# A single-core encoder step whose opening is rebuilt: turned inputs, sums of squares as products, a halved first quarter

## The chip, the core and the metric

The kernel runs on one core of one Trainium2 chip. The metric is the time on the device in microseconds, from the start of the program to its end; lower is better.

## What is computed

One layer of a streaming encoder over 384 rows (256 of a prompt, 8 x 16 of samples) of width 2048. Cut to what the change touches:

```python
mod = einsum('bd,de->be', silu(c), w_ada) + b_ada        # c: 9 rows of 2048; w_ada: 2048 x 6144
shift, scale, gate = split(mod, 3)
h = rmsnorm(x, ln_gain) * (1 + scale[:, None]) + shift[:, None]
proj = einsum('btd,de->bte', h, w_in)                    # then latent attention, sparse attention,
out = einsum('bte,ed->btd', y, w_out)                    # gated norms, and the output projection
```

So every product with `w_in` needs h, and the quarter of h for 512 columns of the model width needs the shift and scale of those columns. Such a quarter takes all 2048 rows of `w_ada`, for 512 columns of the shift and 512 of the scale.

## The kernel before

All weights are streamed from HBM once, packed on the host into "units" of 128 partitions x 1024 floats (512 KB). `units()` writes out by hand the order in which TensorE works through them; `loads()` gives the order of their transfers, all issued by SyncE (SP) on one queue. A unit of the modulation goes into a ring of 8 slots (`araw`), every other one into a second ring of 8 (`raw`); SP waits, in order, until the slot's earlier unit has been used.

- Modulation units ("ada"): 16 per quarter of the width, four quarters. A unit is one 128-row block (kt) of `w_ada` with 512 columns of shift and 512 of scale; TensorE multiplies the silu of c with it (`products`, L1761, 4 matmuls of 256 columns, which the trace shows as 8 records).
- Dense units ("kb", the keys; "ga", the gates of group A; "ckv" and so on): columns of `w_in`. Each is split into a high and a low part: ScalarE copies it to `w_hi` (L957), VectorE subtracts (L1280), and TensorE multiplies high by high, high by low and low by high, with h split the same way: 18 matmuls of 512 columns for a key unit (L1780), 24 of 384 for a gate unit (L1791). Splits are written three units ahead in ScalarE's and VectorE's programs.
- Between the modulation units of the second to fourth quarter stand three or four dense units each, so that TensorE has work while w_ada streams. A key unit of index k covers the width blocks 2k and 2k+1 and needs h of those; a "ga" unit covers four blocks.

`plan()` hangs further steps on the units, in the same order on every engine. At the end of a quarter q: `modT` (ScalarE copies the bank into `modA`, TensorE turns it, VectorE adds the bias, L1326 to L1330), then `h` for its two pairs of blocks (VectorE L1342 for the samples, ScalarE L1039 for the prompt, then the copy to `hT_hi`), then `hl` (`hT_lo`, L1351). `hT_ready` counts the finished blocks and the early key and gate units wait for it. Each engine runs its own program strictly in this order.

The opening. SP first issues c (two transfers), an identity matrix, and x in three transfers of 1 MB with rows on partitions; then the units. GpSimd issues six small loads, the gains among them. TensorE turns c; ScalarE takes its silu into `cs`. ScalarE and VectorE each square half of every row tile with a running sum (`xsq`); `xr` forms 1/rms with row-wise scalars, a diagonal of it times a matrix of ones spreads it over the partitions (`rb`, L1827), and then TensorE turns x in twelve steps of four blocks (L1836), one between any two modulation units, and VectorE multiplies each with 1/rms on its way to `xsT` (L1310). A last small transposition brings the gains into `gcol`.

## Time and profile before

| | us |
|---|---|
| median of 3 runs | 921.27 (920.39 to 922.1) |
| the profiled execution, its own time | 921.53 |
| its span (first to last instruction) | 919.7 |
| TensorE busy | 885.2 (96%) |
| VectorE, ScalarE, GpSimd busy | 413.8, 321.7, 121.8 |

The span is what the trace covers; 1.8 us of the execution lie around it. Times in rows are from the span's start. The page gives shares over the whole span; what bounds a stretch is read from the timeline and the waits of that stretch. In the timeline a row is one instruction or several equal ones in sequence (x8 is eight records), and the bracket tells how long the engine had stood idle and who released it.

### The profile page before, as it was taken

The numbers are of one execution on the slowest core, as the hardware profiler recorded it, in microseconds if no ns is written. First come the engines' busy times: TensorE is split into PE (matmuls) and PEld (weight loads), VectorE is DVE, ScalarE is ACT, GpSimd is POOL, SyncE is SP. The second block draws the span as 40 slices with busy tenths as digits, with TensorE's granted clock in tenths as the row PEclk, the third lists the DMA queues.
The fourth block names the chain that finished last, engine by engine and source line by source line (L and its number), as shares of the span: only waits on it lengthen the run. The fifth ranks groups of instructions, "written<-read, shape, count | busy, mean of one in ns | idle before, by whom it ended". The sixth has DMA issues, their size and how long they took to land.

```text
span 919.7 us, 13678 instructions
## 1 busy us (share of the span) xinstructions
PE 885.2 (96%) x5533; PEld 766.1 (83%) x5533; DVE 413.8 (45%) x850; ACT 321.7 (35%) x600; POOL 121.8 (13%) x192
## 2 busy tenths in 40 slices
PE   3799999999999999999999999999999999999996
PEld 1376788999998688888999888888988899778886
DVE  3522343336422145443332476138645466677362
ACT  3222343333421234222331353234234345554252
POOL 1000003101200000112220400003002224440000
PEclk9799999999999999999999999999999999999999
DMA  8999957475443222556552667547878843793413
GB/s 339 409 408 409 407 199 221 157 238 168 150 136 105 69 75 86 172 165 238 166 157 88 216 228 248 185 159 218 315 246 254 262 141 110 264 303 120 138 53 131
DMA packets 53599, 187.43 MB, mean 204 GB/s; under 512 B 7872, under 2 KB 8568, under 8 KB 52384
## 3 DMA queue, kind: packets, MB, share of 16 engines
q1 hardware_dynamic: 39488, 141.32, 43.7%
q0 software_dynamic: 13904, 44.71, 15.2%
q8 instruction: 44, 0.72, 0.3%
q10 hardware_dynamic: 144, 0.52, 0.1%
q14 instruction: 19, 0.16, 0.1%
HBM read 175.93 MB, written 12.69 MB: 205 GB/s over the span
## 4 chain that ended last, share of the span: by engine, by line
PE 82%; DVE 3%; ACT 2%; issue 1%; POOL 0%; DVEq 0%; ACTq 0%; POOLq 0%
PE proj L1791 33%; PE proj L1780 27%; PE proj L1810 2%; PE proj L1761 2%; PE bankO L1889 2%; PE bankO L1898 1%; PE bankS L1810 1%; DVE w_lo L1280 1%; PE bankS L1952 1%; PE bankO L1979 1%; PE bankO L1971 1%; PE bankO L1970 1%; PE bankO L1939 1%; PE bankS L1780 1%; PE bankS L1995 1%
## 5 line engine op out<-in xcount | busy, mean ns | idle before, releaser
L1280 DVE TENSOR_TENSOR w_lo<-raw,w_hi 128x1024 fp32r<-128x1024 f32 (+2 forms) x164 | 197.5, 1211 | 239.7 <-ACT w_hi L957 239.0
L957 ACT ACTIVATE w_hi<-raw 128x1024 fp32r<-128x1024 f32 (+2 forms) x164 | 167.2, 1026 | 183.7 <-PE proj L1780 104.3
L1791 PE MATMUL proj<-hT_hi,w_hi 128*128 128x384 f32 x608 | 210.7, 347 | 0.0
L1791 PE MATMUL proj<-hT_hi,w_lo 128*128 128x384 f32 x608 | 203.7, 335 | 0.0
L1791 PE MATMUL proj<-hT_lo,w_hi 128*128 128x384 f32 x608 | 203.4, 335 | 0.0
L1780 PE MATMUL proj<-w_hi,hT_hi 128*128 128x512 f32 (+2 forms) x464 | 178.5, 385 | 2.3 <-DVE w_lo L1280 1.5
L1780 PE MATMUL proj<-w_hi,hT_lo 128*128 128x512 f32 (+2 forms) x464 | 174.1, 375 | 0.0
L1780 PE MATMUL proj<-w_lo,hT_hi 128*128 128x512 f32 (+2 forms) x464 | 173.9, 375 | 0.0
L1791 PEld LDWEIGHTS proj<-hT_hi,w_hi 128*128 128x128 f32 x608 | 114.2, 188 | 9.4 <-issue 8.2
L1791 PEld LDWEIGHTS proj<-hT_lo,w_hi 128*128 128x128 f32 x608 | 114.3, 188 | 0.6 <-issue 0.2
L1791 PEld LDWEIGHTS proj<-hT_hi,w_lo 128*128 128x128 f32 x608 | 114.1, 188 | 0.0
L1780 PEld LDWEIGHTS proj<-w_hi,hT_hi 128*128 128x128 f32 x464 | 87.6, 189 | 19.9 <-DVE w_lo L1280 4.4
L1780 PEld LDWEIGHTS proj<-w_hi,hT_lo 128*128 128x128 f32 x464 | 87.4, 188 | 14.9
L1780 PEld LDWEIGHTS proj<-w_lo,hT_hi 128*128 128x128 f32 x464 | 87.7, 189 | 14.5 <-issue 0.7
L1761 PE MATMUL bankO<-araw,cs 128*32 128x256 f32 x512 | 36.7, 407 | 14.8 <-DMA araw<-in_units 13.7
L1761 PEld LDWEIGHTS bankO<-araw,cs 128*32 128x32 f32 x512 | 13.8, 112 | 30.5 <-issue 15.9
L1090 ACT ACTIVATE probs<-probs,stat 128x128 f32<-128x128 f32 (+2 forms) x40 | 17.7, 442 | 58.0 <-DVE stat L1412 49.4
L957 ACT ACTIVATE stage<-proj 128x384 f32<-128x384 f32 (+1 forms) x26 | 12.4, 538 | 28.2 <-PE proj L1791 11.9
L1402 DVE COPY knT<-bankO 128x256 f32<-128x256 f32 x8 | 3.4, 425 | 33.9 <-PE bankO L1889 33.9
L1506 DVE COPY qlT<-bankO 128x512 f32<-128x512 f32 x8 | 5.5, 692 | 29.1 <-PE bankO L1971 29.1
L929 POOL DMA_DIRECT2D out_k_p<-stage x2 | 1.5, 750 | 127.6 <-ACT stage L957 127.6
L1761 PE MATMUL proj<-raw,cs 128*32 128x256 f32 x256 | 18.2, 387 | 0.0
(371 smaller groups left out, 1036.2 us busy)
## 6 DMA issues: line engine op xcount, KB each, us to landing
raw<-in_units SPq DMA_DIRECT2D x184, 512.0 KB, 3.6
araw<-in_units SPq DMA_DIRECT2D x64, 512.0 KB, 9.1
kcT<-in_dsa_k_t POOLq DMA_DIRECT2D x8, 512.0 KB, 5.9
vc<-in_cache_dsa_v POOLq DMA_DIRECT2D x8, 512.0 KB, 5.0
gate_scratch<-stage POOLq DMA_DIRECT2D x8, 384.0 KB, 3.3
raw<-in_units SPq DMA_DIRECT2D x8, 336.0 KB, 4.4
raw<-in_units SPq DMA_DIRECT2D x8, 320.0 KB, 4.5
x_sb<-in_x_prompt SPq DMA_DIRECT2D x2, 1024.0 KB, 6.8
```

The costliest lines, as they stand in the source:

```text
L957: return nc.scalar.activation(out, in_, func, scale=scale, **kw)
L1090: ins = nc.scalar.activation(probs[:, e, p0:p0 + w], probs[:, e, p0:p0 + w] if src is None else src, ACT.Exp, bias=stat[:, 32 + 2 * e + s0 ...
L1280: V.tensor_tensor(w_lo[:, SLOT[u], 0:w], raw_of(u)[:, 0:w], high(u)[:, 0:w].bitcast(F32), ALU.subtract).then_inc(lo_ready, 1)
L1761: ins = mm(banks[0][32 * g:32 * (g + 1), 0:256], cs[:, k, :], cols, start=first, stop=final)
L1780: ins = mm(banks[t][:, 0:ncol], a[:, kt, rows], w[:, n, :], start=first and n == m == 0, stop=final and n == per - 1 and m == 2)
L1791: ins = mm(banks[blk][:, 0:TOK], w[:, n, cols], a[:, kt, :], start=first and n == m == 0, stop=final and n == per - 1 and m == 2)
L1810: ins = mm(out[:, part], a[:, kt, rows], w[:, n, part], start=k == n == m == 0, stop=last and n == 1 and m == 2)
L1889: ins = mm(out[:, 0:SEQ], wukT[:, h_ % 2, q, :], ckvT[:, q, 0:SEQ], start=q == 0, stop=q == CB - 1)
L1898: ins = mm(out[:], ckvT[:, q, P * t:P * (t + 1)], wuvT[:, q, 512 * g:512 * (g + 1)], start=q == 0, stop=q == CB - 1)
L1939: ins = mm(out[:, P * q:P * (q + 1)], wuk[:, h_ % 2, P * q:P * (q + 1)], qnT[:, h_, SEQ:TOK], start=True, stop=True)
L1952: mm(out[:, 0:NKEY], qlT[:, q, b, :], ckvcT[:, b % 3, q, :], start=q == 0, stop=False)
L1970: mm(out[:, cols], ckvc[:, b % 4, cols], probsT[:, b % 2, 0:P], start=True, stop=False)
```

## The change

- x and c are laid out turned on the host (model width on partitions). x comes in four transfers of 768 KB straight into `xsT`, after one for c; the identity and the gains, now turned too, follow behind the second unit. GpSimd's four loads of gains go; its last two wait until x has landed. TensorE's turning of c, of x (48 transpositions) and of the gains goes.
- The sums of squares: ScalarE and VectorE square the 16 blocks (1536 or 768 elements at a time, `xsq`), TensorE adds them up by 16 products with ones in four column groups (`xss`), VectorE copies, one more product with ones spreads the sum (`rb`), ScalarE takes the root of 128 x 384 and VectorE the reciprocal of 128 x 384. x is then scaled by pairs of blocks (`xm`, 8 instructions of 128 x 768 on VectorE) between the other steps.
- The first quarter of the modulation is cut into two halves ("ade", 8 units each, each unit two row blocks by 256 + 256 columns). `modT`, `h` and `hl` follow each half with one pair of blocks; the first pair can so be ready after 8 units.
- The two "ga" chunks of the opening become one, "gp", of 8 units of two row blocks by 512 columns, with four banks.
- The order of units: dense units stand now at positions 10, 14, 22 and 29 of the first 36 (from 0), where they stood at 20, 25, 30 and 35. From position 36 on the kinds stand as before, a "gp" for each "ga". Dense units are loaded 3 or 4 positions early, not 6. In `loads()` the last modulation unit is number 76 (from 0) both times.

The diff, cut to its core ("..." marks what is left out):

```diff
...
-MQ = 4
+MODS = [("ade", 0), ("ade", 1), ("ada", 1), ("ada", 2), ("ada", 3)]
+MOD_BLOCKS = [(0, 2), (2, 4), (4, 8), (8, 12), (12, 16)]
+MOD_OF_PAIR = [0, 1, 2, 2, 3, 3, 4, 4]
...
-    out = [("ada", q, 1, 1) for q in range(4)]
-    out += [("kb", 0, 2, NT), ("ga", 0, 4, 2), ("ga", 1, 4, 2), ("ckv", 0, 2, NT), ("m0", 0, 2, NT), ("m1", 0, 2, NT)]
+    out = [("ade", e, 2, 1) for e in range(2)] + [("ada", q, 1, 1) for q in range(1, 4)]
+    out += [("kb", 0, 2, NT), ("gp", 0, 2, 4), ("ckv", 0, 2, NT), ("m0", 0, 2, NT), ("m1", 0, 2, NT)]
...
-    keys, first, second = of("kb", 0), of("ga", 0), of("ga", 1)
-    out = of("ada", 0)
-    for q in range(1, 4):
-        ada = of("ada", q)
-        out += ada[:4] + [keys[2 * q - 2]] + ada[4:8] + [first[q - 1]] + ada[8:12] + [keys[2 * q - 1]] + ada[12:]
-        out.append(second[q - 1])
-    out += [keys[6], keys[7], first[3], second[3]]
+    keys, gates = of("kb", 0), of("gp", 0)
+    half = of("ade", 1)
+    out = of("ade", 0) + half[:2] + [keys[0]] + half[2:5] + [gates[0]] + half[5:]
+    ada = of("ada", 1)
+    out += ada[:4] + [keys[1]] + ada[4:10] + [gates[1]] + ada[10:]
+    for q in range(2, 4):
+        ada, n = of("ada", q), 2 * q - 2
+        out += ada[:4] + [keys[n]] + ada[4:8] + [gates[n]] + ada[8:12] + [keys[n + 1]] + ada[12:] + [gates[n + 1]]
+    out += [keys[6], keys[7], gates[6], gates[7]]
...
-    for u in [u for u in order if CHUNKS[UNITS[u][0]][0] != "ada" and u < last + 3]:
+    first = UNITS.index((CHUNK_OF["ade", 1], 0))
+    second = UNITS.index((CHUNK_OF["ada", 1], 0))
+    last = UNITS.index((CHUNK_OF["ada", 3], KT - 1))
+    for u in [u for u in order if CHUNKS[UNITS[u][0]][0] not in ("ade", "ada") and u < last + 3]:
         at = order.index(u)
         order.remove(u)
-        order.insert(max(first, at - AHEAD), u)
+        order.insert(max(first, at - (3 if u < second else 4)), u)
...
+        return [u + LEAD] if u + LEAD != FIRST_UNIT["kb", 0] else []
...
+        elif kind == "gp":
+            mine = [3, 4, NPB + 1, NPB + 2]
...
-    put(0, ("xsq", 0), ("xsq", 1), ("xsq", 2), ("xr", 0))
+    put(0, ("xsq", 0), ("xsq", 1), ("xsq", 2), ("xsq", 3))
+    put(0, ("xss", 0), ("xss", 1), ("xss", 2), ("xss", 3))
     put(1, ("rb", 0))
-    run(1, "xT", 6, 2)
-    run(2, "xS", 6, 2)
-    put(13, ("gains", 0))
-
-    for q in range(4):
-        u = LAST_UNIT["ada", q]
-        put(u, ("modT", q))
-        for kind in ("h", "hl"):
-            put(u, (kind, 2 * q), (kind, 2 * q + 1))
+    put(4, ("xm", 0))
+    put(9, ("xm", 1))
+    for m in range(2, 8):
+        put(8 + 2 * m, ("xm", m))
+
+    for n, mod in enumerate(MODS):
+        u = LAST_UNIT[mod]
+        pairs = [m for m in range(KT // 2) if MOD_OF_PAIR[m] == n]
+        put(u, ("modT", n))
+        if n == 0:
+            put(u, ("first_hi", 0))
+        put(u, *(("h", m) for m in pairs))
...
+        put(u, *(("h", m) for m in pairs))
+        if n == 0:
+            put(u, ("first_lo", 0))
+        put(u, *(("hl", m) for m in pairs))
...
-        sp.dma_start(c_rows[:, 0, :], i["c_sample"].rearrange("j (k p) -> (j k) p", p=P)).then_inc(sem("c_in"), 16)
-        sp.dma_start(c_rows[0:KT, 1, :], i["c_prompt"].rearrange("j (k p) -> (j k) p", p=P)).then_inc(sem("c_in"), 16)
-        sp.dma_start(eye[:], i["c_eye"]).then_inc(sem("eye_in"), 16)
-        for t in range(NT):
-            sp.dma_start(x_sb[:, t, :], x_rows[0][:, t] if t < 2 else x_rows[1]).then_inc(sem(f"x_in{t}"), 16)
-        for u in LOADS:
+        sp.dma_start(c_sb[:], i["c_t"]).then_inc(sem("c_in"), 16)
+        for at_, u in enumerate(LOADS):
+            for n in {0: (0, 1, 2, 3)}.get(at_, ()):
+                blocks = slice(4 * n, 4 * n + 4)
+                sp.dma_start(xsT[:, blocks, :], i["x_t"][:, blocks, :]).then_inc(sem(f"x_in{n}"), 16)
+            if at_ == 1:
+                sp.dma_start(eye[:], i["c_eye"]).then_inc(sem("eye_in"), 16)
+                sp.dma_start(gcol[:], i["gains_t"]).then_inc(sem("gains_in"), 16)
...
-            load(gains_in[0:16, :], i["ln_gain"][0].rearrange("(k p) -> k p", p=P), "small_in")
-            load(gains_in[16:24, :], i["out_gain_a"][0].rearrange("(k p) -> k p", p=P), "small_in")
-            load(gains_in[24:32, :], i["out_gain_b"][0].rearrange("(k p) -> k p", p=P), "small_in")
-            load(gains_in[32:64, :], i["b_ada"][0, 0:2 * D].rearrange("(k p) -> k p", p=P), "small_in")
+            pool.wait_ge(sem("x_in3"), 16)
...
+        def xsq(n):
+            if n != 1:
+                blocks = slice(4 * n, 4 * n + (2 if n == 3 else 4))
+                act.wait_ge(sem(f"x_in{n}"), 16)
+                copy(xsqr[:, blocks, :], xsT[:, blocks, :], func=ACT.Square).then_inc(sem(f"x_sq{n}"), 1)
+
+        def rb(n):
+            filled(act, "rb", n)
+            nc.scalar.activation(rbc[:], bank["T"][:, 0:TOK], ACT.Sqrt, scale=1.0 / (32 * D),
+                                 bias=stat[:, 62:63]).then_inc(free["T"], 1)
+
+        def first_hi(_):
...
+            act.wait_ge(sem("x_scaled"), m + 1)
...
-        copy(cs[:, :, 1:9].rearrange("p k j -> p j k"), bank["S"][:, 0:P].rearrange("p (j k) -> p j k", k=KT),
-             func=ACT.Silu)
-        copy(cs[:, :, 0], bank["S"][:, P:P + KT], func=ACT.Silu).then_inc(sem("cs_ready"), 1)
+        copy(cs[:, :, 0:1 + DB], c_sb[:], func=ACT.Silu).then_inc(sem("cs_ready"), 1)
...
+        def xss(n):
+            if n < 3:
+                return
+            filled(dve, "xss", n)
+            V.tensor_copy(xsum[:], bank["S"][:, 0:TOK]).then_inc(free["S"], 1)
 
         def rb(n):
-            filled(dve, "rb", n)
-            V.tensor_copy(rbc[:], bank["S"][:, 0:TOK]).then_inc(free["S"], 1)
-
-        def turned(kind, n, b, i):
-
-            t, g = i % NT, i // NT
-            emptied(dve, "rb", 0)
-            filled(dve, kind, n)
-            V.tensor_tensor(xsT[:, 4 * g:4 * g + 4, P * t:P * (t + 1)], bank[b][:].rearrange("p (k q) -> p k q", q=P),
-                            rbc[:, P * t:P * (t + 1)].unsqueeze(1).broadcast_to([P, 4, P]),
-                            ALU.mult).then_inc(free[b], 1)
-
-        def xT(n):
-            turned("xT", n, "T", 2 * n)
-
-        def xS(n):
-            turned("xS", n, "S", 2 * n + 1)
+            emptied(dve, "rb", n)
+            link(V.reciprocal(rbc[:], rbc[:]))
+
+        def xm(m):
+            part = xsT[:, 2 * m:2 * m + 2, :]
+            V.tensor_tensor(part, part, rbc[:].unsqueeze(1).broadcast_to([P, 2, TOK]),
+                            ALU.mult).then_inc(sem("x_scaled"), 1)
+
+        def first_lo(_):
+            split(FIRST_UNIT["kb", 0])
...
+            if (kind, j) in MODS[1:] and first:
+                emptied(pe, "modT", MODS.index((kind, j)) - 1)
+            if kind == "gp" and first:
+                emptied(pe, "xss", 3)
+                emptied(pe, "rb", 0)
...
+                for n, g in itertools.product(range(2), range(4)) if kind == "ade" else ():
+                    cols = raw_of(u).rearrange("p (a n) -> p a n", a=2)[:, n, P * g:P * (g + 1)]
+                    ins = mm(banks[0][32 * g:32 * (g + 1), 0:P], cs[:, 2 * k + n, :], cols, start=first and n == 0,
+                             stop=final and n == 1)
...
+        def xss(n):
+            out = take("xss", n, "S")
+            pe.wait_ge(sem(f"x_sq{n}"), 2 if n == 3 else 1)
+            for g in range(4):
+                ins = mm(out[32 * g:32 * (g + 1), 0:TOK], ones[:, 0:32], xsqr[:, 4 * n + g, :], start=n == 0,
+                         stop=n == 3)
+            if n == 3:
+                ins.then_inc(full["S"], 1)
+
...
+            emptied(pe, "xss", 3)
+            mm(take("rb", n, "T")[:, 0:TOK], ones[:], xsum[:], start=True, stop=True).then_inc(full["T"], 1)
...
+    x = np.concatenate([inputs["x_prompt"][0], inputs["x_sample"].reshape(P, D)])
+    c = np.concatenate([inputs["c_prompt"], inputs["c_sample"]])
+    gains = np.concatenate([inputs["ln_gain"][0], inputs["out_gain_a"][0], inputs["out_gain_b"][0],
+                            inputs["b_ada"][0, 0:2 * D]])
+    return {"x_t": x.reshape(TOK, KT, P).transpose(2, 1, 0),
+            "c_t": c.reshape(1 + DB, KT, P).transpose(2, 1, 0),
+            "gains_t": gains.reshape(-1, P).T,
```

## Rows read from the trace of the kernel before

**Rows 1.** The page: the chain that ended last, its share by engine.
```profile
PE 82%; DVE 3%; ACT 2%; issue 1%; POOL 0%; DVEq 0%; ACTq 0%; POOLq 0%
```

**Rows 2.** The chain that ended last, in order: start, us, engine and line.
```profile
97.91 4.38 PE proj L1780 x18
...
117.51 2.11 PE bankS L1791 x12
...
139.40 40.60 PE proj L1780 x198
```

**Rows 3.** Engines by stretch: busy us (instructions), granted clock, DMA share, GB/s.
```profile
9.00:10.00 1.00, 0.00 (x0) 0.00 (x0) 0.00 (x0) 0.00 (x0) 0.00 (x0) 1.00 1.10 311
...
80.00:100.00 20.00, 18.77 (x162) 13.98 (x161) 8.32 (x13) 7.11 (x10) 0.00 (x0) 1.00 1.03 408
...
120.00:140.00 20.00, 20.00 (x100) 17.31 (x99) 6.68 (x7) 9.73 (x15) 2.23 (x4) 1.00 0.45 145
```

**Rows 4.** Timeline, ScalarE: start, us, what, [idle before <-releaser]; weight splits that waited for loads.
```profile
46.49 1.06 ACT L957 ACTIVATE w_hi<-raw 128x1024 fp32r<-128x1024 f32 x1 [3.46 <-DMA raw<-in_units]
...
114.45 1.06 ACT L957 ACTIVATE w_hi<-raw 128x1024 fp32r<-128x1024 f32 x1 [7.87 <-DMA raw<-in_units]
```

**Rows 5.** Timeline of the opening, several engines, same columns.
```profile
2.10 0.91 SPq L688 DMA_DIRECT2D x_sb<-in_x_prompt  x2
...
13.34 1.06 ACT L1024 ACTIVATE sqx<-x_sb 128x1024 f32<-128x1024 f32 x1 [1.18 <-DMA x_sb<-in_x_sample]
...
14.73 2.27 PE L1761 MATMUL bankO<-araw,cs 128*32 128x256 f32 x16 [10.50 <-DMA araw<-in_units]
...
18.61 0.56 DVE L1303 COPY rbc<-bankS 128x384 f32<-128x384 f32 x1 [2.37 <-PE bankS L1827]
19.36 0.64 PE L1761 MATMUL bankO<-araw,cs 128*32 128x256 f32 x8
...
35.02 0.64 PE L1761 MATMUL bankO<-araw,cs 128*32 128x256 f32 x8 [0.64 <-DMA araw<-in_units]
```

**Rows 6.** Timeline from the end of the second quarter's modulation to the next key unit.
```profile
63.84 0.38 ACT L957 ACTIVATE modA<-bankO 128x256 f32<-128x256 f32 x1 [9.68 <-PE bankO L1761]
...
65.31 1.68 DVE L1342 TENSOR_TENSOR xsT<-xsT,modT 128x256 f32<-128x256 f32 x4
...
67.45 0.96 DVE L1351 TENSOR_TENSOR hT_lo<-xsT,hT_hi 128x768 fp32r<-128x768 f32 x1 [0.45 <-ACT hT_hi L957]
...
70.23 2.36 DVE L1280 TENSOR_TENSOR w_lo<-raw,w_hi 128x1024 fp32r<-128x1024 f32 x2
...
71.51 0.50 PE L1780 MATMUL proj<-w_hi,hT_hi 128*128 128x512 f32 x1 [0.76 <-DVE w_lo L1280]
```

**Rows 7.** Granted clock by stretch, around its fall and its rise.
```profile
36.00:37.00 1.00, 0.45 (x2) 0.20 (x2) 0.32 (x3) 0.11 (x1) 0.00 (x0) 0.73 0.99 397
46.00:47.00 1.00, 1.00 (x4) 0.84 (x3) 0.00 (x0) 0.51 (x1) 0.00 (x0) 0.65 1.04 410
```

**Rows 8.** Timeline of TensorE between the first dense units.
```profile
37.62 1.08 PE L1761 MATMUL bankO<-araw,cs 128*32 128x256 f32 x8 [1.01 <-DVE modT L1326]
...
43.70 0.80 PE L1780 MATMUL proj<-w_hi,hT_hi 128*128 128x512 f32 x1
...
49.42 1.93 PE L1761 MATMUL bankO<-araw,cs 128*32 128x256 f32 x32
...
51.28 0.44 PE L1791 MATMUL proj<-hT_hi,w_hi 128*128 128x384 f32 x1
...
55.65 1.93 PE L1761 MATMUL bankO<-araw,cs 128*32 128x256 f32 x32
```

**Rows 9.** Timeline much later: a root, a reciprocal and 16 small matmul records of the same shapes.
```profile
534.92 0.58 ACT L1162 ACTIVATE rstd_y<-bankO,stat 128x384 f32<-128x384 f32 x1 [2.90 <-PE bankO L1985]
...
535.60 2.55 DVE L1523 RECIPROCAL rstd_y<-rstd_y 128x384 f32<-128x384 f32 x1 [1.85 <-ACT rstd_y L1162]
...
693.42 0.64 PE L2078 MATMUL bankO<-vc,probsT 128*32 128x128 f32 x16
```

More of the change, by code:

```diff
@@ L400, in packed_units @@
         dst = out[u, :, 0:per * n].reshape(P, per, n)
-        if kind == "ada":
+        if kind == "ade":
+            for a in range(2):
+                dst[:, :, 256 * a:256 * (a + 1)] = w_ada[:, ks, a * D + 256 * j:a * D + 256 * (j + 1)]
+        elif kind == "ada":
             for a in range(2):
@@ L1009, in evict @@
                 ins.then_inc(proj_free[b], 1)
-        def gains(n):
-            filled(act, "gains", n, "S")
-            copy(gcol[:], bank["S"][:, 0:64]).then_inc(free["S"], 1)
         def bias(n):
@@ L1195, in kl @@
                  bank["T"][:].rearrange("p (h s) -> p h s", s=P)).then_inc(free["T"], 1)
-        steps = {"gains": gains, "bias": bias, "xsq": xsq, "xr": xr, "h": h, "ckn": ckn, "ckT": ckT,
+        steps = {"bias": bias, "xsq": xsq, "rb": rb, "first_hi": first_hi, "h": h, "ckn": ckn, "ckT": ckT,
                  "kiT": kiT_,
@@ L1314, in xT, with xsq @@
-        def xT(n):
-            turned("xT", n, "T", 2 * n)
-        def xS(n):
-            turned("xS", n, "S", 2 * n + 1)
+        def xsq(n):
+            if n % 2:
+                blocks = slice(4 * n + (2 if n == 3 else 0), 4 * n + 4)
+                part = xsT[:, blocks, :]
+                dve.wait_ge(sem(f"x_in{n}"), 16)
+                V.tensor_tensor(xsqr[:, blocks, :], part, part, ALU.mult).then_inc(sem(f"x_sq{n}"), 1)
+        def xss(n):
[3 more added lines that the diff above has]
+            V.tensor_copy(xsum[:], bank["S"][:, 0:TOK]).then_inc(free["S"], 1)
@@ L1320, in modT_ @@
+        def rb(n):
+            emptied(dve, "rb", n)
[5 more added lines that the diff above has]
+        def first_lo(_):
+            split(FIRST_UNIT["kb", 0])
         def modT_(n):
             filled(dve, "modT", n)
-            part = modT[:, :, MQ * n:MQ * (n + 1), :]
@@ L1784, in products @@
             else:
-                for blk in range(2):
+                for blk in range(nb):
                     cols = slice(P * blk, P * (blk + 1))
@@ L1854, in ckT @@
             if t == 0:
-                moved(pe, "ga", 1)
+                moved(pe, "gp", 0)
             out = take("ckT", t, "T")
```

151 lines of the change are left out of this document (50 added, 101 removed), and 2 rows, old and new, of the table STEP_BANKS.

## Prediction, made before the changed kernel ran

> **What bounds the kernel now.** I read the page's chain first, then the chain in order of time, then the stretches, and then the timeline of the opening. The chain is TensorE for 82% [rows 1]. From 97.91 on it is TensorE almost without a break, and from 117.51, the first dense unit behind the last modulation unit, it runs on into 40 us of key-like units and so to the end [rows 2]. A time won or lost before 117.5 therefore comes out at the end one for one, as the stretch from 120 on shows: TensorE busy for 20.00 of 20 us, the transfers at 45% [rows 3]. What is left to ask is when the last modulation unit can be done.
>
> In the opening two things run neck and neck. The transfers stand at 408 GB/s, full, while TensorE is busy for 18.77 of 20 us [rows 3]. Landings can be read where ScalarE waits for a weight: load number 24 (from 0) at 46.49, number 77 at 114.45, so one unit per 1.282 us, and number 76, the last modulation unit, at 113.2 [rows 4]. TensorE finishes it at about 116.6, 2.9 us after landing plus its own half microsecond. So even before, TensorE and not the stream sets the end of this stage, by about 3 us. Of TensorE's own time there: a key unit 4.3 us at full clock [rows 2], a gate unit 4.36 (51.28 to 55.65), four modulation units with their gap 1.86 (49.42 to 51.28) [rows 8].
>
> TensorE begins its first key unit only at 43.70. Until 14.7 it has nothing, then its 20 modulation units come as fast as they land, between the turning of x.
>
> **The change, part by part.**
>
> The start of the stream. x is issued at 2.10 and its last third is there at 13.34, 11.24 us later; the first unit 1.36 after that [rows 5]. After, x goes out behind one transfer instead of three, near 1.15 (issues are 0.4 to 0.5 apart by the same row), so it lands near 12.4. The microsecond from 9 moved 311 GB/s and not 408 [rows 3]; if the small tables that GpSimd loads beside it are the cause, moving them saves 0.2 to 0.4. I take x at 12.0 (bounds 11.2 and 12.8), unit 0 at 13.4. The identity, gains and tables (some 0.16 MB) come later and take 0.4 at 408 GB/s, so later units land 1.0 earlier than before. Number 7 landed at about 24.2 (14.7 plus 7 times 1.355, the spacing up to number 15 at 35.02 [rows 5]), after: 23.2, and number 8 at 24.5. Bounds of this term: 0 to 2 us earlier.
>
> Turning x, c and the gains. 48 transpositions and three small ones leave TensorE, all before 33 us. They stand in a time in which it waits for units anyway: worth nothing by themselves. The cover is the landing of the units, and it stays.
>
> The new norm. Squares of the last x blocks: one instruction of 768 elements, near 0.96 as VectorE's of that size in rows 6, so 13.0. TensorE takes unit 0 first, then the 16 products with ones. Nothing shows this form of 384 columns in four column groups; the bounds are the 8 records of unit 0 at half and at full clock (1.08 and 0.5 to 0.64 per set of 256 columns [rows 5, 8]), times 1.5 and four sets: 3.0 to 6.5. The engine worked from 14.73 to 19.36 before an 8-record unit ran at 0.64 and not 1.1, so I take 5.0: 19.5. Then VectorE's copy 0.56 [rows 5], the spreading product 0.8 (estimated from the same 256-column records), the root of 384 columns 0.58, the reciprocal of 384 columns 2.55 [rows 9], the first scaling 0.96: 25.0. The cost of a reciprocal over 384 columns in place of 3 is 2.4 us, and it lies right beside the modulation's chain, below, so it costs nothing to 0.5.
>
> The first half. Number 7 at 23.2, its products 0.5, then bank, transposition and modulation: 1.47 for a full quarter (63.84 to 65.31 [rows 6]), 1.3 for a half: ready at 25.0. ScalarE has the high part of the first key unit ahead of h (`first_hi`): landed 24.5, 1.06 long [rows 4], 25.6. Then h and the high part, 2.14 (65.31 to 67.45), and `hT_lo` 0.96 [rows 6]: the first key unit can start at 28.7, where before it was 43.70. That is the gain of the change, 15.0 us, and the rest of the sum is what takes it back.
>
> The order behind it. Both kernels have four dense and 32 modulation units among the first 36, and the same kinds from number 36 on. So I follow TensorE to the key unit at position 40, which starts at 71.51 before [rows 6]; what comes after it is equal.
> - First key unit: 28.7. Before, it ran at the half clock for its first part and took 5.7 (43.70 to 49.42 [rows 8]), 1.4 over the full speed. The granted clock had fallen to 0.50 (1.2 GHz) at 36.5, after a stretch in which TensorE was busy for about half of the time, waiting for units; it came back to 1.00 (2.4 GHz) within 46 to 47 [rows 7]. After, the engine is still idler before 28.7. So 5.7: 34.4.
> - Three half-quarter units: 16 records each; such a set took 0.64 [rows 9]; 1.6 with the gap: 36.0. Gate unit 4.36: 40.4. Three more: 42.0.
> - Modulation of the second half 1.3: 43.3. The four units behind it (1.9) are all the work that TensorE now has, for the key unit at position 22 needs this h: 2.14 + 0.96, then one `xm` of 0.96 that stands ahead of its split on VectorE, then the split, 1.2 (half of 2.36 [rows 6]): 5.3. It starts at 48.6. TensorE is idle for some 4 of the 6.6 us since 42.0, less busy than in the stretch that lost the clock before [rows 5, 7], so it starts at half clock: 5.7, 54.3.
> - Six units 2.8, gate unit 4.36, six units 2.8: 64.3. Loads: number 35 is there at 46.49 + 11 x 1.282 - 1.0 = 59.6, early enough.
> - Modulation 1.5, 65.8, and 6.2 from there to the key unit (65.31 to 71.51 [rows 6]): 72.0. Before, this same chain ran under a gate unit, 4.36, and the four units; the new order has only the four. Another 7.7 us with 2.3 of work, another start at half clock, 1.4 again.
>
> In all 72.0 + 1.4 against 71.51: 1.9 us later. How long a rise takes is not one number: 1.4 of loss here, and from 14.73 to 19.36 [rows 5] 4.6 us at half speed, which is 2.3 of loss. I take 1.6 for each of the three, 0.6 more in all: **2.5 us slower**. Bounds: 1.9 - 1.0 (start of the stream at its best) to 1.9 + 2.7 + 1.0.
>
> On this point the Trainium skill has a rule that speaks against the change: "TensorE: Matmul & The Clock Gate", section "HAM oscillation — how this bites in real kernels", says that waits between bursts of matmuls throttle the engine anew, so that each burst begins slow. By that rule both new gaps cost a slow start, as in the sum; by the rows alone one could also hope that the 2 us of products inside each gap hold the clock, which would make the sum about 3 us less.
>
> The rest. Behind position 75 the order is the same. "gp" is evicted in one go with four copies; its wait for the keys' store on ScalarE is one where there were two, and TensorE stood at nothing there: its row from 139.40 is unbroken [rows 2]. Nothing, either way (bounds -0.3 to 0.3). Loads 3 or 4 early in place of 6: a split wants 2.3 us, and TensorE lags the loads by more; nothing. While TensorE is in a gap, the 8 slots stay full and SP waits, so the stream may pause for 1 to 2 us; the last modulation unit lands at 112.2 to 114.2, and TensorE comes to it near 119: covered.
>
> **The sum.** 921.53 (the profiled execution; the median of the runs is 0.26 below it) + 2.5 = 924.0.
>
> **The rivals.**
> - The clock holds in the gaps. For it: the three waits of 0.5 to 0.8 at the ends of the old quarters [rows 6] did not lose it. Against: those were short. Then two starts cost nothing: 924.0 - 3.2 = 920.8.
> - The early start pays. TensorE keeps most of its lead of 15 us (the chains to h are shorter than I make them, or dense work fits in), and the stream becomes the bound: the last modulation unit lands at 112.2, done at 112.7 and not 116.6: 917.6. This is the other side, faster; it decides as soon as the second and third chains are 4 us shorter or covered. For it: a full stream from 10 to 118. Against: in the new order nothing dense stands under either chain.
> - The rises are slow. All three as from 14.73: 0.7 more each, 2.1; and if the norm's chain (reciprocal) ends last, 0.5 more: 926.6.
> - The change does not reach the end at all, because gain and gaps cancel by chance: 921.5.
>
> **How the numbers follow.** Forecast (922.6 to 925.4) 0.40; clock holds 0.20; early start pays 0.18; slow rises 0.15; cancels 0.07. A measurement of this kernel tells about 0.2% from no change, 1.8 us: faster is below 919.4, slower above 923.1. Slower: 0.29 of the forecast and all of the slow rises, 0.44. Faster: 0.17 of the early start and 0.04 of the clock case, 0.21. The rest, 0.35, is the same. The range goes from 917.5 to 927.5: it takes in all cases but the best part of the early start (up to 0.1) and what goes beyond the slow rises (up to 0.08).
>
> **What the profile will show.** The first key unit at 28 to 29.5 (before 43.70). Two gaps on TensorE, near 44 to 49 and 66 to 72, with a `w_lo` split as releaser of the key unit that ends each. PEclk at 0.50 in both gaps and into the key units behind them, whose first products last 0.63 and not 0.39. ScalarE's waits for loads shifted by about -1. The key unit at position 40 at 71.5 to 74. If the gaps are there and the clock is 1.00 in them, the first rival holds; if the key units follow without a gap, my reading of the order is wrong, and the time falls to the stream's bound. If TensorE waits for loads in the third quarter, the stream's pause was under-priced.

## The result, and the profile after

The changed kernel takes 924.28 us (median of nine executions), the kernel before 921.27 beside it (nine, 920.39 to 922.1). The ratio is 1.0026, 95% interval 1.0015 to 1.0036, which is 2.4 us; the two medians lie 3.0 us apart. It is slower by 0.26%, just beyond the 0.2% that can be told from no change; the forecast was 924.0. Its executions took 922.11 to 925.27, but for one in a slow state (1116.97), and such ones are left out of all ratios. The profiled execution took 924.28 with a span of 922.4, where before's had 919.7.

The page's shares of the chain by engine, to be read against [rows 1]:

```profile
PE 82%; DVE 3%; ACT 2%; issue 1%; POOL 0%; ACTq 0%; POOLq 0%; DVEq 0%
```

Nothing of the difference is to be seen there. It is in the chain in order of time (start, us, what):

```profile
100.62 4.38 PE proj L1782 x18
...
142.12 40.60 PE proj L1782 x198
```

The block of 40.60 us is as long as before and starts 2.72 us later [rows 2]; so does the key unit at position 60 (100.62, 2.71 later). The span is 2.7 longer. So all of the loss stands before 100, and it reaches the end one for one. The timeline of the opening, from the first unit to the end of the third key unit, and then ScalarE at the end of the modulation:

```profile
13.20 1.08 PE L1756 MATMUL bankO<-araw,cs 128*32 128x128 f32 x16 [13.20 <-DMA araw<-in_units]
...
14.02 5.21 PE L1828 MATMUL bankS<-xsqr,ones 128*32 128x384 f32 x32
...
21.47 2.55 DVE L1308 RECIPROCAL rbc<-rbc 128x384 f32<-128x384 f32 x1 [1.62 <-ACT rbc L1039]
...
24.93 0.26 DVE L1326 TENSOR_TENSOR modT<-bankO,gcol 128x18 f32<-128x18 f32 x2
...
28.66 0.47 PE L1782 MATMUL proj<-w_hi,hT_hi 128*128 128x512 f32 x1 [0.55 <-DVE hT_lo L1350]
...
42.97 1.93 PE L1763 MATMUL bankO<-araw,cs 128*32 128x256 f32 x32 [0.35 <-DVE modT L1326]
...
48.30 0.50 PE L1782 MATMUL proj<-w_hi,hT_hi 128*128 128x512 f32 x1 [3.40 <-DVE w_lo L1290]
...
54.22 2.80 PE L1763 MATMUL bankO<-araw,cs 128*32 128x256 f32 x48
...
69.92 0.94 PE L1763 MATMUL bankO<-araw,cs 128*32 128x256 f32 x8 [0.63 <-DMA araw<-in_units]
...
71.85 0.79 PE L1782 MATMUL proj<-w_hi,hT_hi 128*128 128x512 f32 x1 [0.99 <-DVE w_lo L1290]
...
78.52 1.93 PE L1763 MATMUL bankO<-araw,cs 128*32 128x256 f32 x32
...
117.40 1.06 ACT L969 ACTIVATE w_hi<-raw 128x1024 fp32r<-128x1024 f32 x1 [5.32 <-DMA raw<-in_units]
119.35 0.38 ACT L969 ACTIVATE modA<-bankO 128x256 f32<-128x256 f32 x1 [0.89 <-PE bankO L1763]
```

The first key unit starts at 28.66, where it was 43.70 [rows 8]: a lead of 15 us. The next two stand behind waits for their own low part (48.30, and 71.85 where it was 71.51 [rows 6]). The third begins with a record of 0.79 us and takes 6.67 (71.85 to 78.52): the lead is gone, and more. "The first gap" below is the wait before 48.30, "the second gap" the waits before 71.85. The same stretches by engine (columns as in [rows 3]):

```profile
29.00:30.00 1.00, 1.00 (x4) 0.83 (x3) 0.56 (x2) 0.79 (x1) 0.00 (x0) 0.58 1.01 401
45.00:48.00 3.00, 0.00 (x0) 0.00 (x0) 2.72 (x3) 2.18 (x3) 0.00 (x0) 1.00 1.03 414
49.00:50.00 1.00, 1.00 (x6) 0.77 (x5) 1.00 (x3) 0.00 (x0) 0.00 (x0) 0.82 1.06 430
50.00:51.00 1.00, 1.00 (x4) 0.80 (x3) 1.00 (x1) 0.00 (x0) 0.00 (x0) 0.50 1.04 418
53.00:54.00 1.00, 1.00 (x6) 0.73 (x4) 0.00 (x0) 0.00 (x0) 0.00 (x0) 0.97 0.18 70
54.00:56.00 2.00, 2.00 (x38) 1.09 (x40) 0.00 (x0) 0.00 (x0) 0.00 (x0) 1.00 0.19 27
56.00:58.00 2.00, 2.00 (x26) 1.42 (x19) 0.00 (x0) 0.00 (x0) 0.00 (x0) 1.00 0.76 277
70.00:71.00 1.00, 0.86 (x8) 0.08 (x8) 1.00 (x2) 0.54 (x1) 0.00 (x0) 0.56 1.04 414
```

TensorE does nothing from 45 to 48 and keeps a granted clock of 1.00 (2.4 GHz) all that time; the fall to 0.50 (1.2 GHz) comes at 49.6, inside the key unit behind the gap. In the second gap the clock falls before the key unit begins. And from 53 to 56 the transfers stand nearly still, at 70 and then 27 GB/s.

### The profile page after: what moved, and what is told of

Same layout as the page of the kernel before. It is cut to its first block, busy times and chain, and to the rows that moved or that the text cites. A ratio compares the mean times of both kernels' runs of the same rounds, so it can differ in the third digit from the quotient of the medians.

```text
span 922.4 us, 13853 instructions
## 1 busy us (share of the span) xinstructions
PE 882.5 (96%) x5642; PEld 769.1 (83%) x5642; DVE 413.5 (45%) x840; ACT 323.1 (35%) x596; POOL 118.9 (13%) x187
## 4 chain that ended last, share of the span: by engine, by line
PE 82%; DVE 3%; ACT 2%; issue 1%; POOL 0%; ACTq 0%; POOLq 0%; DVEq 0%
PE proj L1793 33%; PE proj L1782 27%; PE proj L1812 2%; PE proj L1763 2%; PE bankO L1882 1%; PE bankO L1891 1%; PE bankS L1812 1%; DVE w_lo L1290 1%; PE bankS L1945 1%; PE bankO L1972 1%; PE bankO L1964 1%; PE bankO L1963 1%; PE bankO L1932 1%; PE bankS L1782 1%; ACT w_hi L969 1%
## 5 line engine op out<-in xcount | busy, mean ns | idle before, releaser
L1782 PEld LDWEIGHTS proj<-w_hi,hT_hi 128*128 128x128 f32 x464 | 88.6, 191 | 24.3 <-DVE w_lo L1290 8.4
L1763 PE MATMUL bankO<-araw,cs 128*32 128x256 f32 x384 | 23.9, 386 | 3.3 <-DMA araw<-in_units 1.9
L1756 PE MATMUL bankO<-araw,cs 128*32 128x128 f32 x256 | 8.9, 283 | 15.7 <-DMA araw<-in_units 14.5
L1763 PEld LDWEIGHTS bankO<-araw,cs 128*32 128x32 f32 x384 | 11.1, 109 | 13.7 <-DMA araw<-in_units 3.3
L1756 PEld LDWEIGHTS bankO<-araw,cs 128*32 128x32 f32 x256 | 7.0, 113 | 18.0 <-issue 15.1
```

Of the source, the lines that this page charges most:

```text
L1756: ins = mm(banks[0][32 * g:32 * (g + 1), 0:P], cs[:, 2 * k + n, :], cols, start=first and n == 0, stop=final and n == 1)
L1763: ins = mm(banks[0][32 * g:32 * (g + 1), 0:256], cs[:, k, :], cols, start=first, stop=final)
L1782: ins = mm(banks[t][:, 0:ncol], a[:, kt, rows], w[:, n, :], start=first and n == m == 0, stop=final and n == per - 1 and m == 2)
```

## The experiments

All are edits of the changed kernel, run 7 to 11 times beside the kernel before. They are numbered in the order in which they were planned; 9 is told last. Each ratio is to before in the same set (medians 921.12 for 1 to 4, 921.41 for 5 to 8, 920.9 for 9 to 11) with its 95% interval. Spans and rows are of one profiled execution each; differences between two edits of different sets are of ratios. `UNITS` positions are counted from 0. Load 77 is the transfer behind that of the last modulation unit (load 76); it brings a key unit that is used three positions behind it.

**The cover of the chains.** The theory: the new order lets two chains from modulation to h to key unit stand bare, where before a gate unit lay under them. The rival: the time is set by the stream, or by the clock alone, and a cover changes nothing.

```diff
-    out = of("ade", 0) + half[:2] + [keys[0]] + half[2:5] + [gates[0]] + half[5:]
+    out = of("ade", 0) + half[:2] + [keys[0]] + half[2:] + [gates[0]]
```

Experiment 1, as expected before it ran:

> The changed kernel, with the first early gate unit moved behind the last unit of the second half-quarter (position 17, was 14), so that it lies under the chain modulation, h, key unit. Nothing else is changed and the output is the same. Theory (the gap of 3.4 us on TensorE before the key unit at 48.3, the slow clock that it brings to that unit, 5.9 instead of 4.3, and the stream's pause near 53 to 56 that follows because no slot comes free, are the first half of what the change loses): this key unit starts at 43.7, the stream no longer pauses, the second gap stays: the key unit at position 40 at about 67.8 with a slow clock still; 920.3. Rival 1 (only TensorE's gaps count, the stream has slack): 6.6 us less than the changed kernel, 917.7. Rival 2 (the new norm with its 2.55 us reciprocal sets the opening): no change, 924.3.

920.09 us, ratio 0.9990 (0.9981 to 0.9999), span 918.2. One gate unit three places later, under the chain, gives back 0.36% of the time, 3.3 us: the changed kernel's loss and a little more. The gap before the second key unit is gone, and the third starts at 68.39 instead of 71.85, still behind a gap and with a slow clock (0.50 from 66 to 71). As expected (920.3).

```diff
-    out += ada[:4] + [keys[1]] + ada[4:10] + [gates[1]] + ada[10:]
+    out += ada[:4] + [keys[1]] + ada[4:] + [gates[1]]
```

Experiment 2, as expected before it ran:

> The changed kernel, with the second early gate unit moved behind the last unit of the second quarter (position 35, was 29), under the chain that ends at the key unit of position 40; the first gap stays. Theory: the first gap and its slow key unit pause the stream for 3.9 us, so after this edit the key unit at position 40 waits for its modulation units to land (number 40 at about 69.9) and only the slow clock of that unit goes: 2.4 to 2.7 us less than the changed kernel, 921.6 to 921.9. Rival 1 (the stream has slack, a covered gap counts in full): 4.2 + 2.3 less, 917.8. Rival 2 (norm): 924.3.

924.27 us, ratio 1.0030 (1.0019 to 1.0041), span 922.5: no gain, and a clear miss. Yet the key unit at position 60 starts at 98.72, 1.9 us earlier than in the changed kernel. The chain in order of time, then ScalarE's and TensorE's timeline, show where that went:

```profile
98.72 4.38 PE proj L1782 x18
103.10 1.91 PE bankO L1763 x32
105.53 12.71 DMA raw<-in_units
118.37 0.85 issue
120.08 2.09 PE proj L1793 x12
```

```profile
118.26 1.06 ACT L969 ACTIVATE w_hi<-raw 128x1024 fp32r<-128x1024 f32 x1 [5.35 <-DMA raw<-in_units]
119.22 0.37 ACT L969 ACTIVATE modA<-bankO 128x256 f32<-128x256 f32 x1
...
119.64 0.44 PE L1842 MATMUL bankO<-eye,modA 128*128 128x128 f32 x2 [2.01 <-ACT modA L969]
```

The last modulation bank was done by 117.6 (119.64 less the wait of 2.01), but ScalarE works in order, and in its program the split of load 77 stands ahead of the copy of that bank. Load 77 lands at 118.26, its split takes 1.06, and the copy follows without idle time. So the stage ends by a transfer that nobody needs yet. I had taken the last modulation unit itself as the stream's bound. Here load 77 is 0.9 later than in the changed kernel (117.40); this execution was as far behind at its first key unit already (29.51 against 28.66), where the programs are still the same.

Experiment 3, as expected before it ran:

> Both moves together. Theory: no gap before either key unit, no pause of the stream, and then the stream is the bound: the last modulation unit lands at about 112.3 and is done at 112.8 where the changed kernel has 119.3: 6.4 us less than the changed kernel, 917.8, which is more than the sum of the single moves if these give 4.0 and 2.5 only by chance. Rival 1 (gaps simply add, no bound by the stream): 6.6 + 6.5 less, 911. Rival 2 (norm): 924.3.

Both hunks together: 920.02 us, ratio 0.9987 (0.9977 to 0.9997), span 917.8. TensorE's timeline, then ScalarE's:

```profile
56.04 0.64 PE L1763 MATMUL bankO<-araw,cs 128*32 128x256 f32 x8 [1.92 <-DMA araw<-in_units]
```

```profile
113.58 1.06 ACT L969 ACTIVATE w_hi<-raw 128x1024 fp32r<-128x1024 f32 x1 [5.32 <-PE bankO L1763]
114.55 0.37 ACT L969 ACTIVATE modA<-bankO 128x256 f32<-128x256 f32 x1
```

The key unit at position 60 now starts at 95.69, 3.0 us earlier than with the second hunk alone, but only 0.4 earlier than with the first alone (96.13). TensorE now waits for loads between 52 and 60, ahead of the place of the second gap, which is the likely reason why so little comes of the second cover. And the last bank's copy again stands right behind the split of load 77; with the first hunk alone the same pair stood at 113.99 and 114.96. By the medians the second hunk adds nothing to the first (920.02 against 920.09), and the expected 917.8 is missed by 2.2: the bound is the landing of load 77 plus its split.

**The order against the rest.** This takes the new order out and leaves everything else (turned x and c, the norm by products, the start of the stream):

```diff
-    out = of("ade", 0) + half[:2] + [keys[0]] + half[2:5] + [gates[0]] + half[5:]
+    out = of("ade", 0) + half
...
-    out += ada[:4] + [keys[1]] + ada[4:10] + [gates[1]] + ada[10:]
+    out += ada[:4] + [keys[0]] + ada[4:8] + [gates[0]] + ada[8:12] + [keys[1]] + ada[12:] + [gates[1]]
```

Experiment 4, as expected before it ran:

> The changed kernel with the dense units of the opening back at the places of the kernel before (positions 20, 25, 30, 35); everything else of the change stays: turned inputs, sums of squares as products, the halved first quarter, the joined gate chunk. The first key unit's split goes back to its usual place, too. Theory (the new order alone costs what is lost; the other parts give a stream about 1 us earlier and no chain before the first key unit): first key unit at about 41, chain at position 35 to 40 covered as before, 2.6 us less than the kernel before: 918.7. Rival 1 (the other parts cost time themselves, by the reciprocal or the root of 384 columns): 923 to 925. Rival 2 (the other parts are worth nothing): 921.3.

919.86 us, ratio 0.9987 (0.9977 to 0.9997), span 917.9. The rest of the change alone gains 0.13% (1.2 us, interval 0.3 to 2.1), half of the 2.6 expected, and the new order costs 0.39% of the time on top of it, 3.6 us. Its ScalarE timeline:

```profile
113.63 1.06 ACT L965 ACTIVATE w_hi<-raw 128x1024 fp32r<-128x1024 f32 x1 [5.31 <-DMA raw<-in_units]
114.60 0.37 ACT L965 ACTIVATE modA<-bankO 128x256 f32<-128x256 f32 x1
```

Load 77 is 0.82 earlier than in [rows 4], and the copy again stands right behind its split. This kernel too is bound by that landing.

**The clock in the gaps.** The theory: the slow clock of the two key units is a cost of its own. Products of zeros are added into the bank, on TensorE alone, so that the gaps are full but the chains stay:

```diff
+        fill = {21: 14, 36: 2, 37: 2, 38: 2, 39: 6}
...
+            for g in fill.get(u, 0) * [0, 1, 2, 3]:
+                mm(bank["O"][32 * g:32 * g + 23, 0:P], cs[:, 0, 9:32], ones[:], start=False, stop=False)
```

Experiment 5, as expected before it ran:

> The changed kernel, with products of zeros (23 zero columns of the silu tile times ones, four column groups, 128 columns each) added into the open modulation bank in the two gaps of TensorE: 14 sets behind unit 21, 2 each behind units 36 to 38, 6 behind unit 39. They add nothing to the sums, only work under the waits. Theory (the slow clock in the two key units is a cost of its own, 1.6 and 2.4 us, caused by the idle stretch ahead): both key units run at full clock, 4.3 each. The second then ends 3.9 us earlier; but load number 77 still lands late (about 115.8, its split blocks ScalarE until 116.9), so 2.4 less than the changed kernel, 921.8. Rival 1 (the split of load 77 blocks nothing): 920.4. Rival 2 (the clock falls for another reason, or the fills delay the key units): 924.3 or more.

924.08 us, ratio 1.0029 (1.0017 to 1.0040), where 921.8 was expected: a miss. The profiled execution is the fastest of its seven, 922.94, with a span of 921.1. Its stretches around both gaps:

```profile
46.00:48.00 2.00, 1.76 (x65) 1.49 (x54) 2.00 (x4) 0.72 (x1) 0.00 (x0) 1.00 1.02 408
50.00:52.00 2.00, 2.00 (x11) 1.60 (x10) 0.93 (x1) 0.00 (x0) 0.00 (x0) 1.00 1.04 416
54.00:56.00 2.00, 2.00 (x44) 1.19 (x40) 0.00 (x0) 0.00 (x0) 0.00 (x0) 1.00 0.27 39
71.00:73.00 2.00, 2.00 (x29) 1.52 (x19) 1.27 (x2) 0.92 (x1) 0.00 (x0) 1.00 1.04 416
```

In this execution the clock stays at 1.00 throughout, in the gaps and behind them. (Over the whole kernel it had a mean clock of 0.996; the four executions above 924 had 0.992 to 0.994, so in those it was at 0.50 for longer somewhere.) But the last of the zeros start at 48.98 and push the second key unit back by 1.0 us (it starts at 49.31); the transfers pause all the same, and load 77 comes at 116.86 with its split ahead of the bank's copy. For the first gap this settles nothing, since one cost took another's place.

**Splits ahead of h.** The split of each key unit at a quarter's end is written in front of the scaling of x that it waited behind, as the change does for the first one:

```diff
+EARLY = {n: UNITS.index((CHUNK_OF["kb", 0], k)) for n, k in ((0, 0), (1, 1), (2, 2), (3, 4))}
...
-        return [u + LEAD] if u + LEAD != FIRST_UNIT["kb", 0] else []
+        return [u + LEAD] if u + LEAD not in EARLY.values() else []
...
-        if n == 0:
+        if n in EARLY:
```

Experiment 6, as expected before it ran:

> The changed kernel, order of units unchanged, but the splits of the key units at positions 22, 40 and 60 are put ahead of h on ScalarE and between h and hT_lo on VectorE, as the change does for the first key unit; so the chain from modulation to key unit is 3.1 us and not 5.3 or 6.2. Theory (the uncovered length of the chains is what costs): key unit at 22 starts near 46.3 (was 48.3), the stream hardly pauses, key unit at 40 near 66.8 (was 71.9), bounded by its modulation units' landing; end bounded by load 77 and its split near 114.6: 4.7 us less than the changed kernel, 919.6. Rival (norm or the x loads set the time): 924.3. Rival (slow clock stays in both units): 921.5.

921.09 us, ratio 0.9995 (0.9986 to 1.0005), span 919.6: 0.31% (2.9 us) less than the changed kernel, but 1.5 more than expected. With both gate units' hunks on top of it:

Experiment 7, as expected before it ran:

> Both gate units moved under the chains, and the early splits as well. Theory (with both covered, what is last is no longer TensorE but load number 77, whose split stands on ScalarE ahead of the copy of the last modulation bank): the key unit at 40 starts 2.2 us earlier than with the gate units moved alone, and nothing of it reaches the end: 919.8. Rival (TensorE is still last everywhere): 2.9 us less than with the gate units moved alone, 917.1.

920.05 us, ratio 0.9989 (0.9980 to 0.9999), span 919.3 in a profiled execution of 921.05. As expected (919.8), which says: once the bound is load 77 (113.67 here, the copy at 114.63), a shorter chain adds nothing. The rival, 917.1, is out. The sixth kernel's timeline of TensorE, then its stretches:

```profile
45.98 0.47 PE L1783 MATMUL proj<-w_hi,hT_hi 128*128 128x512 f32 x1 [1.48 <-DVE hT_lo L1351]
...
115.37 0.44 PE L1843 MATMUL bankO<-eye,modA 128*128 128x128 f32 x2 [2.00 <-ACT modA L970]
```

```profile
54.00:56.00 2.00, 2.00 (x14) 2.00 (x13) 0.00 (x0) 0.00 (x0) 0.00 (x0) 1.00 1.02 412
...
114.00:115.00 1.00, 0.00 (x0) 0.00 (x0) 0.00 (x0) 1.00 (x2) 0.00 (x0) 1.00 1.02 406
116.00:118.00 2.00, 2.00 (x9) 2.00 (x9) 1.89 (x7) 1.14 (x3) 0.00 (x0) 0.61 1.03 412
```

Three things are to be seen. With the gap cut from 3.40 to 1.48 us, the second key unit starts 2.3 us earlier and runs at full clock, and the transfers do not pause (412 GB/s from 54 to 56): the gap had made the pause. TensorE has won so much that it now waits for the bank's copy, which stands behind load 77's split: nothing from 113.4 to 115.4. And behind this wait its clock falls to 0.50, so that the gate unit there starts slow. The first experiment's kernel copies that bank at the same moment (114.96, here 114.95) but was busy until shortly before:

```profile
114.00:115.00 1.00, 0.83 (x16) 0.26 (x8) 0.00 (x0) 1.00 (x2) 0.00 (x0) 1.00 1.04 414
116.00:118.00 2.00, 2.00 (x13) 2.00 (x13) 1.89 (x7) 1.14 (x3) 0.00 (x0) 1.00 0.97 387
```

It held 1.00 and starts its block of 40.60 us at 137.95, this one at 139.24: the fall cost 1.3 us. It does not come in every execution, it seems. The ten runs of the sixth kernel lie in two groups, four at 919.96 to 920.58 and six, the profiled one among them, at 921.07 to 921.41. The seventh's profiled execution has the same wait (1.98) and the same fall (block at 138.94), but took 1.0 us more than its median. So the fall is the likely reason for most of the miss; which runs had it was not profiled.

**The split of load 77.** The theory: this split holds up the copy of the last bank. It is now written one unit later, on both engines, so that it stands behind that copy:

```diff
+        last_key = UNITS.index((CHUNK_OF["kb", 0], 7))
+        if u == last_key - LEAD:
+            return []
+        if u == last_key - LEAD + 1:
+            return [last_key, u + LEAD]
```

With the hunk of the second experiment:

Experiment 8, as expected before it ran:

> The kernel with only the second gate unit moved (924.3 measured), with one more edit: the split of the last early key unit (load number 77) is written one unit later on ScalarE and VectorE, behind the copy of the last modulation bank and h. Theory (there the chain of waits goes from load 77, landed at 118.3, over its split on ScalarE to the copy at 119.2, while TensorE was done at 117.4): 1.8 us less, 922.4. Rival (the late copy has another cause, or the modulation units themselves land last): 924.3.

922.09 us, ratio 1.0007 (0.9998 to 1.0017), span 919.9: 0.23% (2.1 us) less than the second experiment, as expected. ScalarE's copy, and TensorE's last modulation unit:

```profile
115.99 0.64 PE L1768 MATMUL bankO<-araw,cs 128*32 128x256 f32 x8 [0.26 <-DMA araw<-in_units]
...
116.69 0.38 ACT L974 ACTIVATE modA<-bankO 128x256 f32<-128x256 f32 x1 [4.77 <-PE bankO L1768]
```

The copy starts as soon as the bank is done, 0.7 after the start of that unit's products, and now the last modulation unit's own load is the bound, though barely (TensorE waited 0.26 for it). On the changed kernel as it is:

Experiment 10, as expected before it ran:

> The changed kernel with only that one edit, the split of load 77 written one unit later. In the changed kernel the split ended at 118.46 and the copy of the bank waited for TensorE until 119.35, so theory: no change, 924.3. Rival (the late split is worth 1.8 us wherever it is put): 922.5.

923.11 us, ratio 1.0027 (1.0018 to 1.0036), span 921.2: by the ratio the same as the changed kernel (1.0026); by the medians its distance to before is 2.2 where that had 3.0. The rival, 1.8 us less, lies outside the ratio's interval. So there TensorE is the bound, as expected, and load 77 is not. Its stretches behind the first gap, behind the second, and in the key unit after that:

```profile
50.00:52.00 2.00, 2.00 (x7) 1.63 (x6) 2.00 (x3) 0.00 (x0) 0.00 (x0) 0.61 1.03 418
...
71.00:73.00 2.00, 0.67 (x9) 0.19 (x9) 1.92 (x2) 1.21 (x2) 0.00 (x0) 1.00 1.02 408
73.00:75.00 2.00, 2.00 (x9) 1.66 (x10) 1.22 (x1) 0.51 (x1) 0.00 (x0) 1.00 1.04 414
```

Here the clock held 1.00 across the second gap, and the key unit at position 40 ran at full speed; in the changed kernel's profile it did not. The two programs are the same up to there, so whether it falls differs from one execution to the next. The changed kernel's runs spread over 3.2 us where before's spread over 1.7. The next experiment was to give the mean price of it, the same kernel with zeros in the second gap alone:

```diff
+        fill = {36: 2, 37: 2, 38: 2, 39: 6}
```

Experiment 11, as expected before it ran:

> As the kernel before it in this list, with products of zeros in the second gap only (2 sets of four behind units 36, 37, 38, which wait for their loads, 6 behind unit 39). They end before the key unit at 40 can start. Theory: the granted clock stays at 1.00 through the gap and the key unit takes 4.3 in place of 6.7 us, and nothing else takes the time back (the last modulation unit lands near 116.1): 2.3 us less than the changed kernel, 922.0. Rival (the slow clock is only a sign of the wait and hides under the loads): 924.3.

922.22 us, ratio 1.0014 (1.0005 to 1.0023), span 919.8: 1.2 us less than experiment 10 by the ratio, 0.9 by the medians. That is half of the 2.3 expected, and the intervals of the two ratios overlap a little. So the second gap's clock is worth about 1 us in the mean over executions, if that; the profiled executions do not show it, since both were fast behind the second gap. They differ in the first gap, in which nothing was filled in:

```profile
50.00:52.00 2.00, 2.00 (x11) 1.60 (x10) 2.00 (x3) 0.00 (x0) 0.00 (x0) 1.00 1.02 404
```

The wait was 3.40 us as in the changed kernel, and the key unit behind it was fast. So these two executions give a price for the first gap's slow start. The chains in order of time, experiment 10's and then this one's:

```profile
140.86 40.60 PE proj L1787 x198
```

```profile
139.31 40.60 PE proj L1787 x198
```

Both start the key unit at position 22 at nearly the same time (49.38 and 49.30), leave it at 55.36 and 53.64, and come to the block 1.55 us apart: the first gap's slow start reached the end almost whole, in this one pair. Last, both covers, early splits and the late split together:

Experiment 9, as expected before it ran:

> Both gate units moved under the chains, the early splits, and the split of load 77 written one unit later. Theory (with the gate units moved and the early splits alone, 920.0, the chain of waits went over load 77 and its split to the copy of the last modulation bank at 114.6, while TensorE was ready near 112.3; load 76 lands at about 112.4): the copy near 113.0, 1.6 us less: 918.4. Rival (another wait is right behind): 920.0.

919.15 us, ratio 0.9979 (0.9970 to 0.9988), span 917.5. This version is faster than both kernels, though 0.75 slower than expected. TensorE is bound by the stream in the second quarter already, as in experiments 3 and 7:

```profile
56.75 0.64 PE L1769 MATMUL bankO<-araw,cs 128*32 128x256 f32 x8 [1.90 <-DMA araw<-in_units]
...
60.61 1.08 PE L1769 MATMUL bankO<-araw,cs 128*32 128x256 f32 x8 [0.20 <-DMA araw<-in_units]
```

It waits for one load after the other, and a set of 8 records takes 1.08 and not 0.64 at the end: its clock has fallen here too, ahead of a gate unit.

## Why the prediction came out right, point by point

- **Where the time is set.** From the start of the block of 40.60 us on, a time lost reaches the end one for one in every kernel: span less that start is 780.3 to 780.5 in all thirteen profiles. From the copy of the last modulation bank to the block it is 22.8 to 23.0 us in eleven of them, and 24.3 in the sixth and seventh experiments, where the clock fell behind the wait for that copy. So "before 117.5" was too early a mark: behind it a slow clock can still cost time.
- **Start of the stream, norm.** In the profiled execution this came out as predicted: 13.4 for unit 0, 5.0 for the products with ones, 2.55 for the reciprocal, modulation at 25.0; measured 13.20, 5.21, 2.55, and 25.4. The norm's chain did end last, by 0.6, where its bound was 0.5: TensorE had turned the bank by 24.30, VectorE, busy with the first scaling, came to it at 24.93. The 5.0 was partly luck: in the profiles of the experiments the same products took from 3.8 (the second) to 5.2 (the fifth), and where they took 4.1 or less, VectorE waited for the bank and not the bank for VectorE. The fourth experiment puts a worth of 1.2 us on all that is not order.
- **First key unit.** 28.7 predicted, 28.66 measured. Its duration was 5.9 against 5.7, but the clock was not low before it, as I had it: it was 1.00 at its start and fell at 29.2. That was one execution: in the profiles of all experiments but the fourth (which moves the unit) and the fifth, the clock was at 0.50 when this unit started, as I had it. In four of them (1, 2, 9, 10) the unit also starts later, at 29.5 to 29.9, since the load of its weights, number 8, is there about 1.2 later (its split starts at 25.3 to 25.7, not 24.16).
- **First gap.** Key unit at 48.6 predicted, 48.30 measured, released by `w_lo` as foretold; the slow start cost 1.6 (48.30 to 54.22 against 4.3). One of the prediction's signs failed: the clock is not 0.50 in this gap but only behind it, and the unit's first products are short.
- **Second gap.** Modulation at 65.8 against 65.66; key unit at 72.4 with the 1.6 of each rise counted, against 71.85. Its slow start was mis-sized: 2.35 (6.67 less 4.33, the full-speed unit of these rows) and not 1.6. The sum's 1.6 leaned on a rise of 4.6 us read from record lengths at 14.73 [rows 5]; the clock column of that trace reads 1.00 from 13 to 22, so it does not show that rise. Too late by 0.5 in one term and too little by 0.75 in the other: the sum, 2.5, and the measured 2.7 agree closer than their terms, which is luck.
- **The clock rule.** The rows show a slow start behind both gaps in the changed kernel, behind only the first in the tenth experiment, and behind neither in the profiled execution with zeros in them. The Trainium skill says in "TensorE: Matmul & The Clock Gate", section "HAM oscillation — how this bites in real kernels", that waits between bursts throttle the engine anew; the traces agree in six of eight unfilled gaps of these two kinds (both of the changed kernel, the first in experiments 2, 8 and 10, the second in experiment 1), and not in the other two (the tenth experiment's second, the eleventh's first). The rival "clock holds" (920.8) was thus partly real: it is the likeliest reason why the changed kernel's runs fall into three at 922.1 to 923.0 and five at 924.2 to 925.3. Where in a run the clock was low only a profiled execution shows; the mean clock of each run (0.991 in the three, 0.989 to 0.991 in the five) points that way but doesn't settle it.
- **The pause of the stream.** I said 1 to 2 us and covered. At 408 GB/s, the stretches from 53 to 58 lost 0.83, 1.87 and 0.64 us, 3.3 in all, and load 77 lands at 117.40 where without the new order it landed at 113.63, 3.8 later. Under-priced, then, and with it the sign "waits for loads shifted by about -1" failed: at load 77 ScalarE's wait ends 2.95 later than before (114.45). The gap starts the pause, and the slow unit behind it lengthens it: with the same wait but a fast unit, experiment 11 kept 367 GB/s from 56 to 58, where experiment 10 had 63. It was covered, though only just: load 77 was split by 118.46, and the bank's copy started at 119.35.
- **The stream's bound.** This step was wrong. I took 2.9 us of slack on the last modulation unit's landing. The experiments show another bound: landing of load 77, plus its split (1.06), plus the copy. In the kernel before that is 115.5 against 116.64 (the copy's start), a slack of 1.1 and not 2.9. It did not touch the forecast, since the changed kernel's TensorE is later than that; but the rival "early start pays", at 917.6, asked for second and third chains 4 us shorter or covered. In the third experiment both were covered, and the time stopped at 920.0.
- **Changed nothing, slow rises.** The first is excluded by the interval. The second had the right mechanism for one of the three rises (2.35) and, in the profiled execution, for the norm's chain.

What stays open: why the clock falls behind one wait of 3.40 us and not behind another of the same length. And what the slow starts, the waits and the pause each cost at the end was not separated over many runs: for the first gap there is one pair of executions (1.55 us), the fifth experiment filled that gap but moved the key unit too, and covering or shortening a chain removes all three at once.

## What to carry to other kernels

Starting the bottleneck engine earlier gains only what the next dependent chains let through: before moving dense work to the front, list which chain it was hiding where it stood, and leave something under each. Then look at what stands in an in-order engine's program ahead of the step that ends a stage: a prefetch's conversion there ties the stage to a transfer that is not yet needed, and moving it one place was worth 2.1 us where TensorE was no longer the bound, and nothing where it was. And look at what an engine that gets ahead of its stream does with its lead: here it waited 2 us, its clock fell behind the wait, and 1.3 us were given back.

## What the runs showed of the hardware

- The granted clock follows idleness late: with TensorE idle from 44.9 to 48.3 it stayed 1.00 and fell at 49.6 in the midst of dense work. It then stayed at 0.50 to about 53 though the engine was busy all the time. The key unit behind this gap took 1.6 us more than at full speed, the one behind the second gap 2.35.
- With small products of zeros in both gaps (TensorE busy for 1.76 of 2 us from 46 to 48) it read 1.00 from 44 to 77 in the one execution profiled.
- After the same wait of 3.40 us the next key unit ran slow in four profiled executions (the changed kernel, experiments 2 and 10; 3.39 in experiment 8) and fast in one (experiment 11).
- 16 products of squares with ones, over 384 columns in each of four column groups (the profile groups them as 32 records), took 5.21 us in the changed kernel's profile, mostly in steps of 0.64 us, and 3.8 to 5.2 in the experiments' profiles.
